# A two-layer hybrid attention trunk: index projections first, all low halves on VectorE

## What is computed

```python
proj = jnp.einsum('bsd,dn->bsn', h, w_in)
dq, dk, dv, dg, sq, sk, sv, sg, iq, ik, iw = jnp.split(proj, SPLIT_OFFSETS, axis=-1)
oa = diff_attention(rope(dq), rope(dk), dv, lam)          # softmax 0 - lam * softmax 1, 4 heads
oa = rms_norm(oa, subln_w, SUBLN_EPS) * (1.0 - lambda_init)
oa = oa * silu(dg)
ob = dsa_attention(rope(sq), rope(sk), sv, rope(iq), rope(layer_norm(ik)), iw * c) * silu(sg)
y = jnp.einsum('bsm,md->bsd', concatenate([oa, ob]), w_out)
return x + rms_norm(y, post_w, NORM_EPS)
```

## Time and profile before

| | us |
|---|---|
| median of 3 runs (323.68 to 323.72) | 323.70 |
| the profiled execution, its own time | 323.95 |
| span of the profile, first to last instruction | 322.1 |
| PE busy | 306.8 |
| PE idle while waiting for another engine, after its start | 7.9 |
| from PE's last matmul to the end of the span | 5.7 |

### The profile page before, as it was taken

How to read it: one execution, slowest core, us unless ns; L and a number is a source line. 1 busy time by engine, 2 the same in 40 slices (tenths; PEclk the granted TensorE clock), 3 DMA queues, 4 the chain that set the end, 5 groups by cost and what they waited for, 6 DMA issues and landing times.

```text
span 322.1 us, 4379 instructions
## 1 busy us (share of the span) xinstructions
PE 306.8 (95%) x1580; PEld 252.5 (78%) x1580; DVE 234.5 (73%) x473; ACT 163.0 (51%) x283; POOL 119.9 (37%) x121
## 2 busy tenths in 40 slices
PE   8999999799899999999999999979989999999992
PEld 7788888578677888888887888857767788888881
DVE  2864278989999995753788605898999999667143
ACT  3877375455277455701755627444736563572101
POOL 2834568805320801151063214972352062115011
PEclk9999999999999999999999999999999999999998
DMA  6995986653434039261009494946323501600011
GB/s 208 394 402 181 368 287 255 209 186 130 130 130 132 1 111 327 85 194 68 0 1 347 127 351 162 325 136 258 130 82 103 177 34 25 236 2 0 0 67 65
DMA packets 27269, 51.75 MB, mean 161 GB/s; under 512 B 3312, under 2 KB 3312, under 8 KB 27248
## 3 DMA queue, kind: packets, MB, share of 16 engines
q1 hardware_dynamic: 26960, 51.46, 46.5%
q10 hardware_dynamic: 288, 0.01, 0.1%
HBM read 50.42 MB, written 1.05 MB: 160 GB/s over the span
## 4 chain that ended last, share of the span: by engine, by line
PE 63%; DVE 24%; ACT 5%; POOL 2%; DMA 2%; issue 2%; SPq 0%; DVEq 0%; POOLq 0%; ACTq 0%
PE bank_a L374 10%; PE bank_a L378 10%; PE bank_a L383 10%; PE bank_a L535 7%; PE bank_s L535 6%; DVE w_lo L863 6%; PE bank_t L354 4%; PE bank_o L514 3%; PE bank_a L395 3%; DVE ik L932 3%; ACT w_hi L666 3%; DVE work L967 3%; DVE top L966 2%; DMA xt_pbuf<-in_x_t 2%; DVE xt_pbuf L984 2%
## 5 line engine op out<-in xcount | busy, mean ns | idle before, releaser
L666 ACT ACTIVATE w_hi<-w_raw 128x2048 fp32r<-128x2048 f32 (+1 forms) x46 | 82.1, 1784 | 38.5 <-PE bank_a L383 31.8
L863 DVE TENSOR_TENSOR w_lo<-w_raw,w_hi 128x2048 fp32r<-128x2048 f32 (+1 forms) x36 | 79.0, 2202 | 31.0 <-ACT w_hi L666 30.6
L374 PE MATMUL bank_a<-w_hi,h_hi 128*128 128x512 f32 x256 | 72.4, 405 | 0.0
L378 PE MATMUL bank_a<-w_hi,h_lo 128*128 128x512 f32 x256 | 68.8, 391 | 0.4 <-DVE h_lo L880 0.4
L383 PE MATMUL bank_a<-w_lo,h_hi 128*128 128x512 f32 x256 | 68.6, 390 | 0.0
L378 PEld LDWEIGHTS bank_a<-w_hi,h_lo 128*128 128x128 f32 x256 | 48.0, 188 | 11.2 <-DVE h_lo L880 0.8
L383 PEld LDWEIGHTS bank_a<-w_lo,h_hi 128*128 128x128 f32 x256 | 48.1, 188 | 10.2
L374 PEld LDWEIGHTS bank_a<-w_hi,h_hi 128*128 128x128 f32 x256 | 45.2, 188 | 10.7 <-issue 2.2
L1246 POOL TENSOR_TENSOR w_lo<-w_raw,w_hi 128x2048 fp32r<-128x2048 f32 (+1 forms) x10 | 38.7, 3874 | 22.0 <-ACT w_hi L666 22.0
L1259 POOL TENSOR_TENSOR rt<-nat,tab 128x256 f32<-128x256 f32 x10 | 8.6, 863 | 79.3 <-ACT nat L714 79.3
L730 ACT ACTIVATE xt_pbuf<-xt_pbuf,st 128x128 f32<-128x128 f32 (+1 forms) x48 | 21.3, 444 | 24.5 <-DVE st L984 24.5
(11 more groups left out here) (170 smaller groups left out, 478.8 us busy)
## 6 DMA issues: line engine op xcount, KB each, us to landing
w_raw<-in_w_in SPq DMA_DIRECT2D x34, 1024.0 KB, 5.2
w_raw<-in_w_out SPq DMA_DIRECT2D x8, 1024.0 KB, 5.2
w_raw<-in_w_in SPq DMA_DIRECT2D x4, 512.0 KB, 8.5
prm<-in_rows SPq DMA_DIRECT2D x2, 769.0 KB, 8.2
xres<-in_x SPq DMA_DIRECT2D x2, 512.0 KB, 12.5
out<-xres SPq DMA_DIRECT2D x4, 256.0 KB, 2.3
w_raw<-in_w_in SPq DMA_DIRECT2D x4, 144.0 KB, 8.1
xt_pbuf<-in_x_t SPq DMA_DIRECT2D x1, 512.0 KB, 8.5
```

What stands on the lines that cost most here:

```text
L374: pe.matmul(bank, h_hi[:, HALF * half + kk, tok], whi[:, kk, :], start=half == 0 and kk == 0, stop=False)
L378: pe.matmul(bank, h_lo[:, HALF * half + kk, tok], whi[:, kk, :], start=False, stop=False)
L666: act.activation(unit(w_hi, u), unit(raw, u), ACT.Copy).then_inc(hi_done.sem, 1)
L863: dve.tensor_tensor(unit(w_lo, u), unit(raw, u), unit(w_hi, u).bitcast(F32), ALU.subtract).then_inc(lo_done_dve.sem, 1)
```

## The change

- Chunks come in the order IQ, DG, TAIL, SG, then as before: TAIL is groups 4 and 5 and SG groups 6 and 7. PE starts with IQ, and the index logits of the second block stand one half earlier.
- DVE makes all 24 low halves of a layer. POOL makes none and no longer multiplies the gate; the sub-norm weight is a column of the `x_t` array and goes into DVE's drain of the turned mixer output (`drain_mix` for T_MD0 and T_MD1), by a `tensor_scalar` and a `scalar_tensor_tensor` in place of a copy and a `tensor_tensor`.
- The turned x is loaded in five pieces instead of three, the first of 274 columns instead of 528, and the opening goes by quarters. `positions` and `freqs` are loaded by SP, behind seven loads. 10 identity matmuls instead of 18. The first ACT table is that of the sine, which now runs before the first `move`.
- DVE's order changes: in the first choice a low half comes after four rounds, the eight rounds of the second choice have other neighbours, and low halves 7, 11, 15, 19 and 23 are put in.
- At the layer change, ACT squares y of block 1 before and between the splits of x, DVE makes the low half of unit 1 before it drains x and that of unit 2 after `weight_y`, and POOL's root for block 0 of the next layer comes last.

The diff, cut to its core:

```diff
-WARM_UP = 18
+WARM_UP = 10
 HALF = KT // 2
-PRE_N = DEPTH * KT
+PRE_N = DEPTH * KT + DEPTH
 XT_N = PRE_N + KT * SEQ
...
-DG, SG, IQ, TAIL, DQ, DK, SQ, SK, DV, SV = range(10)
-COLUMNS = [(3, WIDTH), (7, WIDTH), (8, WIDTH), (9, IDX_DIM + IDX_HEADS), (0, WIDTH), (1, WIDTH),
+IQ, DG, TAIL, SG, DQ, DK, SQ, SK, DV, SV = range(10)
+COLUMNS = [(8, WIDTH), (3, WIDTH), (9, IDX_DIM + IDX_HEADS), (7, WIDTH), (0, WIDTH), (1, WIDTH),
            (4, WIDTH), (5, WIDTH), (2, WIDTH), (6, WIDTH)]
 CHUNKS = len(COLUMNS)
...
-LO_POOL = (7, 11, 15, 19, 23)
-LO_DVE = tuple(u for u in range(UNITS) if u not in LO_POOL)
...
+            cuts = [0, x_at(1, 0)] + [x_at(0, FIRST_TILES * q) for q in range(1, 4)] + [XT_N]
+            def turned(i):
+                sp.dma_start(xt[:, cuts[i]:cuts[i + 1]], x_t[:, cuts[i]:cuts[i + 1]]).then_inc(xt_landed[i], 16)
+            turned(0)
             sp.dma_start(piece(raw, 0, 0), weights(0, 0)[:, 0:FIRST_TILES, :]).then_inc(piece_landed[0], 16)
-            sp.dma_start(xt[:, one:two], x_t[:, one:two]).then_inc(xt_landed[1], 16)
+            turned(1)
+            turned(2)
             sp.dma_start(piece(raw, 0, 1), weights(0, 0)[:, FIRST_TILES:HALF, :]).then_inc(raw_landed[0].sem, 16)
-            sp.dma_start(xt[:, two:XT_N], x_t[:, two:XT_N]).then_inc(xt_landed[2], 16)
+            turned(3)
             sp.dma_start(piece(raw, 1, 0), weights(0, 1)[:, 0:FIRST_TILES, :]).then_inc(piece_landed[1], 16)
+            sp.dma_start(pos_i[:, :], positions).then_inc(small_landed, 16)
+            sp.dma_start(frq[:, :], freqs.to_broadcast([P, NF])).then_inc(small_landed, 16)
+            turned(4)
             sp.dma_start(piece(raw, 1, 1), weights(0, 1)[:, FIRST_TILES:HALF, :]).then_inc(raw_landed[1].sem, 16)
             for u in range(2, RING):
...
                 tail_products()
-                first(8)
+                first(6)
                 tail_back()
-                second(8)
+                second(6)
                 turn_nat(T_IQ, 0, 1)
-                first(9)
-                second(9)
+                first(7)
+                second(7)
                 pe.wait_ge(ik_ready.sem, ik_ready.at(layer, 1))
                 turn(T_IK, [ik2[:, b, :, :].rearrange("p t d -> p (t d)") for b in range(BLOCKS)])
-                first(10)
+                first(8)
                 pe.wait_ge(t_drained.sem, t_drained.at(layer, T_IK + 1))
                 index_logits(0, 0, range(4))
+                second(8)
+                index_logits(2, 1, (0, 1))
+                first(9)
+                index_logits(4, 1, (2, 3))
+                second(9)
+                first(10)
                 second(10)
-                index_logits(2, 1, (0, 1))
                 first(11)
                 turn_nat(T_DQ, 1, 2)
-                index_logits(4, 1, (2, 3))
                 second(11)
...
+                if layer == 0:
+                    act.wait_ge(angles_ready, 1)
+                    act.activation(trig[:, 4:6, :], trig[:, 2:4, :], ACT.Sin).then_inc(trig_ready, 1)
                 move(0)
...
-                square_y(0)
+                square_y(0, 0)
+                square_y(0, 1)
                 if layer < DEPTH - 1:
                     act.wait_ge(out_unit_used.sem, out_unit_used.at(layer, 1))
@@ -826,28 +816,34 @@
                     split_hi(layer + 1, 1)
                     act.wait_ge(out_unit_used.sem, out_unit_used.at(layer, 3))
                     split_hi(layer + 1, 2)
+                square_y(1, 0)
+                if layer < DEPTH - 1:
                     x_hi(layer + 1, 0)
+                square_y(1, 1)
+                if layer < DEPTH - 1:
                     square_x(layer + 1, 0)
-                square_y(1)
-            act.dma_start(pos_i[:, :], positions).then_inc(small_landed, 16)
-            act.dma_start(frq[:, :], freqs.to_broadcast([P, NF])).then_inc(small_landed, 16)
             act.wait_ge(neg_half_ready, 1)
-            act.activation(spare, neg_half[:, 0:1], ACT.Silu)
+            act.activation(spare, neg_half[:, 0:1], ACT.Sin)
...
+                        link(dve.tensor_scalar(dst_hi[part], src, weight, None, ALU.mult))
+                        ins = dve.scalar_tensor_tensor(out=dst_lo[part], in0=src, scalar=weight, in1=dst_hi[part].bitcast(F32),
+                                                       op0=ALU.mult, op1=ALU.subtract)
+                    ins.then_inc(t_drained.sem, 1)
...
                 split_lo(layer, 6)
+                split_lo(layer, 7)
                 split_lo(layer, 8)
+                index_key()
+                drain_pair(T_IQ, iqT)
                 split_lo(layer, 9)
+                drain(T_IK, ikT[:, :])
                 split_lo(layer, 10)
-                index_key()
+                split_lo(layer, 11)
                 if layer == 0:
                     dve.wait_ge(causal_ready, 1)
-                drain_pair(T_IQ, iqT)
-                split_lo(layer, 12)
-                drain(T_IK, ikT[:, :])
-                split_lo(layer, 13)
                 index_sum(0, 0, (0, 2, 4, 6))
                 index_sum(1, 0, (1, 3, 5, 7))
                 index_sum(2, 1, (0, 2))
                 index_sum(3, 1, (1, 3))
+                split_lo(layer, 12)
+                index_sum(4, 1, (4, 6))
+                index_sum(5, 1, (5, 7))
+                choose(0, 4)
+                split_lo(layer, 13)
+                choose(0, 4)
+                mask_unchosen(0)
                 drain_pair(T_DQ, dqT, DIFF_QK ** -0.5)
                 split_lo(layer, 14)
-                index_sum(4, 1, (4, 6))
-                index_sum(5, 1, (5, 7))
-                choose(0, 8)
-                mask_unchosen(0)
+                choose(1, 3)
                 drain_pair(T_DK, dkT)
-                choose(1, 3)
+                split_lo(layer, 15)
                 mask_scores(6, 0, 4, causal[:, P:SEQ])
                 mask_scores(7, 0, 4, causal[:, P:SEQ])
-                split_lo(layer, 16)
+                choose(1, 2)
                 dve.wait_ge(lam_exped.sem, lam_exped.at(layer, 1))
                 link(dve.tensor_tensor(neg_lam, lam_e[:, 1:2], lam_e[:, 0:1], ALU.subtract))
                 link(dve.tensor_tensor(neg_lam, neg_lam, param("lam_init"), ALU.subtract))
@@ -1091,24 +1094,24 @@
                 mask_scores(8, 1, 2, causal[:, :])
                 mask_scores(9, 1, 2, causal[:, :])
-                split_lo(layer, 17)
+                split_lo(layer, 16)
                 drain_pair(T_SQ, sqT, E ** -0.5)
                 combine(8, 1, 2, 0)
                 drain(T_PD0, pT[:, 0, :])
                 mask_scores(10, 1, 2, causal[:, :])
                 mask_scores(11, 1, 2, causal[:, :])
-                choose(1, 2)
-                combine(10, 1, 2, 2)
-                drain(T_PD1A, pT[:, 1, :])
                 choose(1, 3)
                 mask_unchosen(1)
+                drain(T_PD1A, pT[:, 1, :])
+                split_lo(layer, 17)
+                combine(10, 1, 2, 2)
                 drain_pair(T_SK, skT)
                 split_lo(layer, 18)
                 drain(T_PD1B, pT[:, 2, :])
                 mask_scores(12, 0, 4, work[0][:, :])
...
+                dve.wait_ge(subln_ready.sem, subln_ready.at(layer, 1))
+                drain_mix(T_MD0, m_hi, m_lo, 0, subln)
                 gate_diff(1)
...
                 drain_mix(T_MS0, h_hi, h_lo, 0)
+                split_lo(layer, 23)
                 gate_dsa(1)
                 weight_y(0)
                 residual(0)
                 drain_mix(T_MS1, h_hi, h_lo, 1)
                 if layer < DEPTH - 1:
                     split_lo(layer + 1, 0)
+                    split_lo(layer + 1, 1)
                     drain_x(layer + 1, 0)
-                    split_lo(layer + 1, 1)
+                weight_y(1)
+                if layer < DEPTH - 1:
                     split_lo(layer + 1, 2)
-                weight_y(1)
                 residual(1)
...
                 if layer:
                     root_x(layer, 1)
+                else:
+                    rotary_tables()
+                rope(IQ, IDX_HEADS, HD, 0)
                 pool.wait_ge(prm_landed.sem, prm_landed.at(layer, 16))
-                link(pool.tensor_scalar(subln, subln, param("one_minus"), E ** 0.5, ALU.mult, ALU.mult))
+                pool.tensor_scalar(subln, subln_in[:, layer:layer + 1], param("one_minus"), E ** 0.5, ALU.mult, ALU.mult).then_inc(subln_ready.sem, 1)
+                pool.wait_ge(ik_var.sem, ik_var.at(layer, 1))
+                link(pool.tensor_scalar(ik_e, ik_mv[:, 1:4:2], LN_EPS, None, ALU.add))
+                pool.tensor_tensor(ik_r, ik_e, neg_half[:, 0:2], ALU.pow).then_inc(ik_rstd.sem, 1)
+                rope(DQ, 2 * HEADS, HD, 0)
+                rope(DK, 2 * HEADS, HD, 0)
+                rope(SQ, HEADS, HS, 2)
+                rope(SK, HEADS, HS, 2)
                 for b in range(BLOCKS):
-                    pool.wait_ge(proj_moved.sem, proj_moved.at(layer, place(layer, DG, b) + 1))
```

(29 more changed lines are left out.)

216 lines of the change are left out of this document (101 added, 115 removed).

## The result

The changed kernel takes **314.52 us** (median of 4 runs, 313.65 to 315.26) where the kernel before takes 323.71 (4 runs, 323.68 to 323.84): a ratio of 0.9715, 95% interval 0.9698 to 0.9732. The profiled execution took 314.57 us for a span of 312.8, so terms are read from that span against 322.1.

The account below looks back on a forecast made before the run. TensorE was taken as nearly full, busy 306.8 of 322.1 us, so only its idle time can be won. Terms −3.5 − 2.9 − 0.5 − 0.4 + 0.4 − 1.0 + 0.9 = −7.0 took 323.7 to 316.7 us; range 315.0 to 319.9.

Parts of the forecast that it names:

- the key: TensorE's wait behind the index key, whose VectorE scalings GpSimd's low half held: −1.75 us in each layer, 3.5 in all.
- DK and SQ: TensorE's waits for the drains of DK and SQ: DK −1.45 us in each layer, SQ −0.5 for both.
- The cap of unit 2: Opening: unit 2 lands at 16.57, its low half ends at 20.8, so TensorE can gain 1.06 us; −1.0 taken.
- the rotation tables: Layer 0: tables ready at 31, IQ's rotation done at 39.3, TensorE wants it at 38.4: +0.9 us, ends 0 and 2.5.
- unit 17: Tightest new place, VectorE's low half with 0.3 us of slack: +0.2 us in each layer, ends 0 and 1.7.
- The rule of the Trainium skill: Of VectorE and GpSimd on the shared pair, the first to begin holds it: some 0.5 us more in each layer, 317.7.
- the layer change: TensorE's wait for a subtraction beside GpSimd's product on the gate, which is gone: −0.4 us.
- VectorE "near 250 us": Sign in the changed profile: VectorE takes on 18 us of low halves and is busy for about 250 us, 80%.
- The slow opening: Rival: ten identity matmuls end before the clock rises to 2.4 GHz, opening products run slow: 318.5 us; chance 0.10.
- Starved rotations: Rival: low halves hold GpSimd's rotations of IQ, DK and SK; each held step from the second costs 2 us: 327; chance 0.06.
- The gain was not taken back: Rival: VectorE late at unit 17 by 1.5 us in each layer, tables cost 2.5: 321 us; chance 0.13.
- The waits did not stay: Rival: TensorE's waits stay since something unseen, not the key, ends them: 323.7 us; chance 0.03.

Follow-up runs that it names:

- experiment 2: Changed kernel with the low half of unit 9 back on GpSimd beside the index key, in both layers: 319.65 us.
- experiment 3: Kernel before, its order kept, with all low halves on VectorE: 321.57 us, ratio 0.9931.
- experiment 4: Changed kernel with unit 17's low half behind the combination of the last differential probabilities instead of ahead of it, in both layers: 318.57 us.
- experiment 1: Identity matmuls: kernel before with 10 instead of 18, ratio 1.0048; changed kernel again 314.98 us, with 18 instead of 10 315.19, with 13 314.69.
- experiment 6: Changed kernel with the loads of positions and freqs put behind units 2 and 3: 318.97 us.

## Why the prediction was right and wrong

**Right: the direction, and the mechanism of the key.** A low half of GpSimd held VectorE's scalings, and with it went the key's wait (experiment 2). The key gave 3.76 us (3.5 forecast) and was ready 2.8 us ahead (2.7 forecast). For DK and SQ the low halves are a part only: moved alone they leave 1.0 and 2.7 us of waits (experiment 3), and the order takes the rest. The cap of unit 2 held as written (−0.80 for −1.0), and the landing was 16.57 as before.

**Wrong: the two costs of the new order, +0.9 and +0.4.** This is the step that failed. They came out as 0 and 0.15, and make 1.15 of the missing 2.3 us. For the rotation tables I had them ready at 31 and three of four steps held, done at 39.3 against a need at 38.4. The tables were ready at 29.7 and two steps were held: 36.28 against 38.63, slack 2.3. At unit 17 the mask took 0.29 as I had it. From the turn ahead of it to SK's turn TensorE needs 6.01 us instead of 5.94, and in layer 1 6.01 instead of 5.93. I priced the doubt: a rotation step did fall beside the low half, and it was the step that stood still (2.67 us), since it had begun 0.35 us later. The rule of the Trainium skill named in the forecast would have said so for this order of starts; the 0.5 us that I worked out from it belongs to a step that begins first. Such a step was there too, but it had only 0.27 us left when the low half began, and the low half took 2.42 us instead of 2.28. That is most of why the slack is 0.1 and not 0.3. Experiment 4 shows how near it was: one move of 1.86 us of small steps costs 3.6.

**Wrong: the size of small waits.** SQ −0.88 for −0.5, the key −3.76 for −3.5, the layer change −0.74 for −0.4, and −0.55 in a stretch where the view showed no wait at all and I had +0.4. A wait in the view begins where the matmul before ends, and that end is modelled: four matmuls are shown as 1.07 us and the next four start after 0.91. So the first 0.16 us of each wait are not in the view, and a wait shorter than that does not show. The −0.55 has its place: from SK's turn to the first products of the probabilities TensorE needed 5.25 us and needs 4.95, in layer 1 5.26 and 4.98, and before, SK's drain stood there behind a mask held until 113.17. With unit 17 counted apart, these four terms gave 1.7 us more than forecast. The balance of the missing 2.3 us is 0.9 + 0.25 + 1.7, less 0.3 for DK and 0.2 for the opening.

DK gave less, 2.59 for 2.9. Before, the scores started 2.52 us behind the four matmuls ahead of them; now it is 1.01, which is what this switch takes where nothing waits too (1.00 at 91.89 before). So DK's wait itself gave 1.51 a layer. The new wait for its rotation takes back 0.14 of that, and the rest is that logits and turn now stand apart, which is argued from the starts alone.

**Wrong: the low end of the range.** An opening that gains 2 and no wait at unit 17 make 316.7 − 1.0 − 0.4 = 315.3, not the 314.9 that I wrote. With my own lower end for the rotation tables, 0, the terms reach 314.4, below the measured 314.52. So the range left out the good end of just the term that failed.

**Wrong, and without effect: VectorE "near 250 us".** It is 237.4. 234.5 + 18 is 252.5, so nothing of what it was to lose had been taken off. With the key's scalings (8.6 less) and the masks (5.0 less) it is 239.

**The rivals.** The slow opening costs 1.6 us with the old loads (experiment 1), and no run shows a cost with the new ones. Starved rotations occurred in small: one held step of DK's rotation costs TensorE 0.14 us a layer. I had called one held step covered. It leaves no slack, so a second one would by the forecast's figure cost its full 2 us; that wasn't tried. The gain was not taken back, though 0.1 us of slack at unit 17 is all there is between the two. The waits did not stay.

## What to carry to other kernels

When an engine's work is taken off a pair that holds each other, count the time that the other engine stood still as well as the time of the work: 19.9 us of low halves cost VectorE 2.9. Price a wait by the starts of the matmuls on either side, not by the idle time shown, and let the range's good end go beyond the view. An opening that waits for one landing gains nothing from an earlier start: find that landing first, and try it in pieces. Where a range is put together from terms, add up the good ends of all of them.

## What the runs showed that I had not expected

- **The runs of the changed kernel differ by 1 to 1.6 us**, those of before by 0.16 to 0.66. With 18 identity matmuls they differ by 0.47, but with 10 and the layer change undone by 0.56, so the clock at the start isn't shown to be the cause. All profiles of the changed opening put the difference ahead of TAIL's turn, and with it goes the landing of unit 2. Why that landing moves is open. In the kernel before, TensorE came 1.06 us after unit 2 was ready, which would cover such a movement; that is argued, not shown. Without a wait for unit 2 the runs still differ by 0.5 to 1.45 us, so it isn't the only cause.
- **A few late load engines set a landing.** Unit 2's packets were done on the first of the sixteen engines at 14.10 us, on twelve by 14.72, and on the last four at 15.06, 15.79, 16.35 and 16.57. With positions and freqs behind units 2 and 3 first and last were 13.78 and 14.88; in ACT's queue at the start 14.40 and 15.81; in the middle 14.02 and 15.34. So 13 KB in packets of 8 and 96 bytes move the last engine by up to 1.7 us. But the kernel before had them at the start of ACT's queue too, and has 14.02 and 16.55: the queue alone doesn't explain it.
- **A wait can cost TensorE its clock.** Behind 3.8 us it was granted 0.53, 2.4 us more (experiment 6); behind 2.15 us 0.76 and 0.67, 1.6 us more (experiment 2); behind 1.43 in the same kernel, 1.60 at unit 17 (experiment 4) and 1.75 at the key in the kernel before, nothing. These are single traces, and the other runs of experiments 2 and 6 suggest that the same wait doesn't cost the same in each execution. Still, the key's wait stood not far from one that once cost nearly twice its length.
